# Parts of a weight chunk ahead of the rotations, sample tokens' value products in two halves, and the second row exchange on ScalarE's DMA queue, in the mixer of a two-layer streaming encoder

## The reference

```python
h = layer_norm(DN_ALPHA * h + 0.5 * swiglu(h, gate0, up0, down0), g0, b0)
p = project(h, pos, w_in, ...)      # qa ka va qb kb vb qi ki wi qc kc vc cq ckv kr
#   rope() on qa ka qb kb qi ki kr; va, vb, vc, wi without
h = layer_norm(DN_ALPHA * h + concat(A(h), B(h), C(h), D(h)) @ w_o, g1, b1)
h = layer_norm(DN_ALPHA * h + 0.5 * swiglu(h, gate1, up1, down1), g2, b2)

def rope(x, pos):                   # x1, x2: the halves of a head
    return concatenate([x1 * cos - x2 * sin, x2 * cos + x1 * sin])
```

## Time and profile before

| | |
|---|---|
| median of 3 runs | 1140.57 us (1140.53 to 1141.63) |
| span of the profiled execution | 1139.0 us |
| between span and median | 1.57 us |
| TensorE busy | 1124.5 us, 99% |
| VectorE busy | 692.7 us, 61% |
| ScalarE busy | 542.9 us, 48% |
| granted TensorE clock | 1.000 |
| DMA, mean over the span | 157 GB/s |

### The profile page before, as it was taken

The page is one execution under the profiler, slowest core; times in us unless marked ns, Lnnn a source line. Parts: engine busy times, 40 slices in busy tenths (PEclk is TensorE's granted clock), DMA queues, the critical chain, the costliest instruction groups (busy, mean ns, idle before and its releaser), DMA issues.

```text
span 1139.0 us, 20704 instructions
## 1 busy us (share of the span) xinstructions
PE 1124.5 (99%) x8576; PEld 1092.3 (96%) x8576; DVE 692.7 (61%) x947; ACT 542.9 (48%) x774; POOL 86.4 (8%) x84
## 2 busy tenths in 40 slices
PE   9999999999999999999999999999999999999998
PEld 8999999988899999999999999999888999999997
DVE  5545444779769745445585554467797596454443
ACT  6343343465655634344373434335657564434332
POOL 1000000100151000000100000010003410000001
PEclk9999999999999999999999999999999999999999
DMA  9544445533433545445445544444534325545431
GB/s 349 186 166 167 153 161 167 168 136 107 152 125 122 202 154 179 151 162 167 149 148 189 181 151 172 151 155 131 179 121 145 139 98 199 182 150 169 151 124 42
DMA packets 29555, 179.37 MB, mean 157 GB/s; under 512 B 3824, under 2 KB 3888, under 8 KB 11824
## 3 DMA queue, kind: packets, MB, share of 16 engines
q1 hardware_dynamic: 27744, 172.54, 44.4%
q0 software_dynamic: 1744, 5.88, 1.5%
HBM read 171.79 MB, written 4.25 MB: 155 GB/s over the span
## 4 chain that ended last, share of the span: by engine, by line
PE 76%; DVE 16%; ACT 3%; issue 2%; DMA 1%; SPq 1%; DVEq 0%; ACTq 0%
PE ps L525 24%; PE ps L526 24%; PE ps L527 24%; DVE w_low L1493 2%; ACT w_high L1157 2%; DVE z L1666 2%; DVE w_low L1506 1%; DMA raw<-weights 1%; DVE x_low L1681 1%; DVE z L1656 1%; DVE score L1816 1%; DVE best L1815 1%; DVE zx_low L1646 1%; SPq L417 1%; DVE score L1780 1%
## 5 line engine op out<-in xcount | busy, mean ns | idle before, releaser
L525 PE MATMUL ps<-x_high,w_high 128*128 128x288 f32 x1536 | 457.6, 298 | 2.0 <-DVE w_low L1493 1.3
L527 PE MATMUL ps<-x_high,w_low 128*128 128x288 f32 x1536 | 452.8, 295 | 0.0
L526 PE MATMUL ps<-x_low,w_high 128*128 128x288 f32 x1536 | 452.5, 295 | 0.0
L1493 DVE TENSOR_TENSOR w_low<-raw,w_high 128x2048 fp32r<-128x2048 f32 (+3 forms) x148 | 322.4, 2180 | 212.1 <-ACT w_high L1157 211.6
L1157 ACT ACTIVATE w_high<-raw 128x2048 fp32r<-128x2048 f32 (+2 forms) x166 | 302.9, 1827 | 114.2 <-PE ps L527 107.4
L525 PEld LDWEIGHTS ps<-x_high,w_high 128*128 128x128 f32 x1536 | 288.3, 188 | 8.4 <-DVE w_low L1493 6.2
L527 PEld LDWEIGHTS ps<-x_high,w_low 128*128 128x128 f32 x1536 | 288.4, 188 | 0.0
L526 PEld LDWEIGHTS ps<-x_low,w_high 128*128 128x128 f32 x1536 | 288.1, 188 | 0.2
L527 PE MATMUL ps<-hid_high,w_low 128*128 128x288 f32 x704 | 208.5, 296 | 0.0
L526 PE MATMUL ps<-hid_low,w_high 128*128 128x288 f32 x704 | 208.3, 296 | 0.0
L525 PE MATMUL ps<-hid_high,w_high 128*128 128x288 f32 x704 | 207.7, 295 | 0.0
(11 more groups left out here) (329 smaller groups left out, 1141.4 us busy)
## 6 DMA issues: line engine op xcount, KB each, us to landing
raw<-weights SPq DMA_DIRECT2D x138, 1024.0 KB, 4.9
raw<-weights SPq DMA_DIRECT2D x16, 768.0 KB, 4.3
raw<-weights SPq DMA_DIRECT2D x4, 968.0 KB, 4.7
raw<-weights SPq DMA_DIRECT2D x6, 512.0 KB, 4.0
raw<-weights SPq DMA_DIRECT2D x8, 256.0 KB, 6.2
relu_l<-rope_x SPq DMA_DIRECT2D x24, 72.0 KB, 2.0
out_k<-kT POOLq DMA_DIRECT2D x2, 864.0 KB, 4.7
raw<-weights SPq DMA_DIRECT2D x2, 640.0 KB, 5.4
```

The costliest lines, as they stand in the source:

```text
L525: pe.matmul(out, wh, xh, start=first, stop=False, skip_group_check=True)
L526: pe.matmul(out, wh, xl, start=False, stop=False, skip_group_check=True)
L527: return pe.matmul(out, wl, xh, start=False, stop=last, skip_group_check=True)
L1493: dve.tensor_tensor(wl, r, wh.bitcast(F32), ALU.subtract).then_inc(low_ready, 1)
```

## The change

Four things change in each of the two layers:

- ScalarE makes the high part of chunk base + 4 (`high_until(base + 5)`) right after `hT`, ahead of the wait for `early_scaled` and of the copies to `rope_x`; VectorE makes `fixed_choice` and the low part of that chunk (`low_until(base + 5)`) ahead of both `rope_first`.
- `sample_tokens` is cut in two. The half for chunk base + 2 runs after `token_major(4)` and signals `v_first_ready`; the other half runs where all of it ran.
- The load of chunk base + 5 waits for `v_first_ready` in place of `v_parts_ready`, and stands ahead of the exchange r = 0 in SyncE's order.
- The exchange r = 1 is issued by ScalarE, after its copies to `rope_x`.

```diff
@@ SyncE
-                if local in (TM_AT + NRAW, TM_AT + NRAW + 1):
+                if local == TM_AT + NRAW:
+                    sp.wait_ge(v_first_ready, l + 1)
+                if local == TM_AT + NRAW + 1:
                     sp.wait_ge(v_parts_ready, l + 1)
...
-                        if local == TM_AT + NRAW:
+                        if local == TM_AT + NRAW + 1:
                             turn_rows(l, 0)
-                            turn_rows(l, 1)
@@ helper, called by turn_rows and by ScalarE
+        def swap_blocks(eng, r):
+            for b in range(4):
+                other = b + 1 - 2 * (b % 2)
+                eng.dma_start(turned(r)[32 * b:32 * b + 32], rope_x[32 * other:32 * other + 32, r % 2, :, :])\
+                    .then_inc(rows_turned[r % 2], 16)
@@ TensorE
-                def sample_tokens():
-                    pe.wait_ge(h_ready, KD * event)
-                    for k in range(KD):
+                def sample_tokens(part):
+                    pe.wait_ge(h_ready, KD * event - 4 * (1 - part))
+                    for k in range(4 * part, 4 * part + 4):
...
-                    mm.then_inc(v_parts_ready, 1)
+                    mm.then_inc(v_parts_ready if part else v_first_ready, 1)
...
                 for k in range(3, KD):
                     token_major(k)
-                sample_tokens()
+                    if k == 4:
+                        sample_tokens(0)
+                sample_tokens(1)
@@ ScalarE, mixer
+                high_until(base + 5)
                 act.wait_ge(h_ready, KD * (3 * l + 1))
                 act.wait_ge(early_scaled, early_before(3 * l) + 1)
...
                 to_rope(1, 0)
                 to_rope(1, 1)
-                high_until(base + 5)
+                act.wait_ge(proj_copied, TILES * l + ROPES[1][0] + 2)
+                swap_blocks(act, 1)
@@ VectorE, mixer
                 early_queries(l)
+                fixed_choice()
+                low_until(base + 5)
                 rope_first(l, 0)
-                fixed_choice()
                 rope_first(l, 1)
-                low_until(base + 5)
                 rope_rest(l, 0)
                 rope_rest(l, 1)
```

More of the change, by code:

```diff
@@ L267, in encoder_program @@
         values_copied = sem("values_copied")
+        v_first_ready = sem("v_first_ready")
         v_parts_ready, v_parts_copied, v_added = sem("v_parts_ready"), sem("v_parts_copied"), sem("v_added")
@@ L414, in turn_rows @@
                     sp.wait_ge(roped, ROPED * l + 3)
[L415 to L418, removed]
+                swap_blocks(sp, r)
             for pair in range(4):
```

## The result

The changed kernel takes **1146.25 us** (median of 4, 1145.68 to 1147.0) against 1140.63 for the kernel before beside it: ratio 1.0045, 95% interval 1.0033 to 1.0056, slower by over 0.2%. The forecast was 1142.2, and its range ended at 1143.8. Its profiled execution took 1145.8 us, with a span of 1144.0 and a granted clock of 1.000, as before. The span grew by 5.0 us.

What follows compares the result with a forecast made beforehand. TensorE is busy 99%, so only its waits on the exchange, load and low-part chain could be won. Per layer: tile 4 -0.71, halves +0.15, tile 6 +1.36, sum +0.8; twice that gives 1142.2 us, range 1139.3 to 1143.8.

Steps and rivals of the forecast that it cites:

- The wait before tile 4 goes: TensorE before tile 4: base + 4's low part is ready before it is asked for, winning 0.71 us a layer.
- 0.11 of restart: TensorE at tile 4: second product comes 0.24 after the first, not 0.13; counted as part of the 0.71 us wait.
- The split, +0.15: Sample tokens in two halves: one more change of tile shape and back costs TensorE 0.15 us, bounds 0 and 0.27.
- The load of base + 5 lands at 244.9, since the queue is served in order: SyncE's queue: load issued at 239.9, takes 5.04 us, leaves the path; exchange r = 0 lands after it.
- The exchange r = 0 behind the load, eight exchanges at 0.20 us, whole at 246.5: SyncE's queue: r = 0 shares engines with all eight transfers and is whole at 246.5, making the high part 0.8 us later.
- Break-even at 245.7, each tenth later costs a tenth: Chain to base + 5's high part: r = 0 whole at 245.7 changes nothing; each tenth earlier wins one, later costs one.
- The keys' first copy at 250.8, just in time: Keys' copy before the indexer's logits: done at 250.8, just before TensorE wants it at 251.1.
- rival B: Exchanges cost 0.28 to 0.31 us each, r = 0 whole at 247.1 to 247.4; 1143.4 to 1144.0 us; chance 0.26.
- Costed at nothing: ScalarE's four issues, 0.63 us each, delay the values' copies, still in time for tile 5; base + 6's load goes earlier.
- the share of lone packets counts their latency: Objection to pricing exchanges at the measured share of 0.45 at 108 GB/s, which gives 0.31 us each.
- r = 1 overtakes and the load gives way: DMA engines turn between queues packet by packet, so ScalarE's r = 1 passes r = 0 and all eight transfers count.

Runs made afterwards that it cites:

- two queues, halves: Kernel before with base + 4 parts ahead, sample tokens split, each exchange issued half by SyncE, half by ScalarE, ahead of the load of base + 5: 1139.06 us.
- r = 1 from ScalarE alone: Kernel before with only exchange r = 1 moved to ScalarE, behind its high part of chunk base + 4; old order, sample tokens whole: 1139.38 us.
- two queues, whole: Kernel before with base + 4 parts ahead, each exchange issued half by SyncE, half by ScalarE, ahead of the load; sample tokens unsplit: 1139.66 us.
- r = 0 ahead, halves: Changed kernel with one move: SyncE issues exchange r = 0 ahead of the load of base + 5; sample tokens stay split: 1139.95 us.
- r = 0 ahead, whole: Changed kernel with exchange r = 0 ahead of the load of base + 5 and sample tokens unsplit, so the load waits for all of them: 1139.86 us.
- parts alone: Kernel before with only ScalarE's and VectorE's parts of chunk base + 4 moved ahead of the rotations; queues and products as before: 1142.06 us.
- r = 1 back behind r = 0: Changed kernel with exchange r = 1 back on SyncE, right behind r = 0, both behind the load of base + 5: 1143.92 us.
- transfers of twice the size: Changed kernel with each exchange as two transfers of 64 partitions in place of four of 32, copied straight, so results differ from the reference: 1146.64 us.
- both on ScalarE's queue: Changed kernel with both exchanges issued by ScalarE, r = 0 first, the load of base + 5 alone on SyncE: 1152.24 us.

## Why the prediction was wrong

**The time goes by the high part of base + 5.** For each kernel, the start of the first product with the sines (reading r = 0) and of that high part, both on before's clock, and the time against the kernel before of the same batch:

| kernel | first sines | high part | shift x 2 | time, us |
|---|---|---|---|---|
| before | 244.89 | 250.41 | | |
| two queues, halves | 243.89 | 249.38 | -2.1 | -1.9 |
| r = 1 from ScalarE alone | 244.88 | 249.62 | -1.6 | -1.6 |
| two queues, whole | 243.89 | 249.81 | -1.2 | -1.7 |
| r = 0 ahead, halves | 245.21 | 249.96 | -0.9 | -1.3 |
| r = 0 ahead, whole | 245.24 | 249.98 | -0.9 | -1.1 |
| parts alone | 244.78 | 251.01 | +1.2 | +0.8 |
| r = 1 back behind r = 0 | 247.14 | 251.87 | +2.9 | +2.7 |
| **changed kernel** | 248.45 | 253.18 | +5.5 | +5.6 |
| transfers of twice the size | 248.96 | 253.69 | +6.6 | +5.3 |
| both on ScalarE's queue | 246.49 | 255.18 | +9.5 | +11.0 |

So the frame of the prediction stands: one chain, from the exchange over VectorE's rotations and the keys' copies to this high part, and two layers. Its shift in layer 0, doubled, gives the time within 0.5 us in eight of ten kernels; in the last two rows it is off by 1.3 and 1.5. Layer 1 has the same shifts to 0.3 us (2.5 for 2.8 in the changed kernel), but for both on ScalarE's queue (5.4 for 4.8).

Step by step:

- *The wait before tile 4 goes.* Right that it goes, too much for it. The second product of tile 4 also starts 0.23 us behind the first where nothing is waited for, so the 0.11 of restart that I put to the wait belongs to the tiles' change of shape. With parts ahead and whole samples the way to tile 4 is 6.17 us, before 6.67 (238.36 to 245.03): 0.50 won, not 0.71.
- *The split, +0.15.* Measured 0.32, over my bound of 0.27. I had costed the change of shape at one end of the half only. After it, the successor starts at 239.59, and the next follows after 0.32 in place of 0.22. Together with the first point: TensorE was at tile 4 0.15 us earlier, not 0.55.
- *The load of base + 5 lands at 244.9, since the queue is served in order.* It was issued when forecast (239.8) but took 6.1 us. In the three kernels where exchanges follow it in its queue it took 6.0 to 6.3. The two loads of the earlier trace rows had shown no such thing: the first of them lost nothing. Its data was hardly later than alone (the last packet starts 4.41 us after the issue, 4.31 in the kernel before), and 15 of its 16 reports had come by 245.13; the last one came at 245.91. The high part asks for the load only at 252.97, so by itself this cost nothing. Whether the DMA engine that was last here was also last with the exchange, the records don't say.
- **The exchange r = 0 behind the load, eight exchanges at 0.20 us, whole at 246.5. This is the step that failed.** It was whole at 248.2, on before's clock 248.4, 1.9 us later. All eight were whole at 248.5, 3.7 us after the load would have landed alone (239.77 + 5.04): **0.46 us each**. Two things went into that. In one queue an exchange cost 0.34, near the 0.31 of my upper bound, so 0.20 was the wrong end: filled engines do not move an exchange's bytes at a load's rate. With it, r = 0 is whole at 247.0, as in the run with r = 1 back on SyncE's queue. The other 0.12 each came with ScalarE's queue, and no term of mine had it. In layer 1 it is less, 0.05 each (0.40 against 0.35). Part of it has nothing to do with later loads: 204 of the 256 packets of both exchanges were through before the first packet of the loads issued from 244.85 on started, at 246.12, and up to there a packet took 0.165 us on average, against 0.148 with one queue. The last 52 did share the DMA engines with these loads; how much each part cost is open.
- *Break-even at 245.7, each tenth later costs a tenth.* Right. 248.4 is 2.7 past it; the high part came 2.77 late and tile 6 2.78. The steps between, 3.8 for the rotations and 0.9 for the copies, came out at 4.73 together (248.24 to 252.97).
- *The keys' first copy at 250.8, just in time.* With the exchange 1.9 later it was done 1.9 later, at 252.48 (252.69 on before's clock), and TensorE waited 1.22 for it before the logits. That lies inside the 2.78, as rival B had it.
- *Costed at nothing.* ScalarE's four issues took 3.07 us, one of them 1.15 and not 0.63; the values' copies at 244.23 were still in time. Right.

Right was thus the mechanism of rival B, which had the exchange at 247.1 to 247.4 and 1143.4 to 1144.0 us. That is nearly the run with one queue (247.0, and 1140.57 + 2.65 = 1143.2 us); the changed kernel adds the price of the second queue. The agreement in r = 0 is in part luck: B had all eight exchanges ahead of its end, and there only its own four were. What I held against B, that the share of lone packets counts their latency, does not bear out: the share was the same in a full queue. A row that warned of company was there, outside. The earlier trace rows covers layer 0 alone, and I said of it "no exchange ever over 2.1". The line's row for the kernel before from 806.5 on reads:

```profile
L417 SPq DMA_DIRECT2D relu_l<-rope_x x8: 512/586/592, 836.3 to 862.4; - x8
...
DMA to landing us min/median/max: 1.9/2.1/3.2
```

The 3.2 is the exchange issued at 862.4. Its company is one packet of 16 KB that loads instructions, the only one of another queue from 862 to 866; it holds one DMA engine from 862.8 to 864.4:

```profile
q8 instruction: 1, 0.02, 2.5%
```

Against that, my best evidence for an undisturbed exchange was eight that had the DMA engines to themselves.

Of the two rules that I weighed, that a second issuing engine saves only sequencer time (the Trainium skill, DMA: Bandwidth & Descriptors, Issuing engines are not separate DMA queues) is borne out by one run and not by the other. Without a load in flight that time was worth 1.6 us, since the load stood behind the issues; with one, moving r = 1 won nothing and cost 3.0 us (5.6 less 2.65). The other, turns between queues, fits the landings of r = 0 and r = 1 that alternate. But what I had made of it, that r = 1 overtakes and the load gives way, did not happen: r = 1 was issued from 241.12 on, and its first packet started at 243.95, when the load's were nearly through (the last at 244.18), beside the first of r = 0 at 243.84.

What stays open is why an exchange's bytes go at 237 and not at 419 GB/s. It is neither the size of its packets nor that it reads on-chip memory: the four stores of the result at the end of the kernel before read it too, in packets of the same 2304 bytes, and these take 0.096 us on average where an exchange's take 0.149. Their window, to be read like those of the earlier trace rows (355 GB/s at a share of 0.94):

```profile
1136.00:1137.00 1.00, 0.00 (x0) 0.00 (x0) 0.00 (x0) 0.45 (x2) 0.00 (x0) 1.00 0.94 355
```

Two differences are left, and no run tells them apart: an exchange has both its ends in on-chip memory, and it covers 32 partitions (64 in the run with larger transfers) where loads and stores cover 128. Open, too, is what makes the second queue dear; no run held the two later loads back. Nor is there a run for the split by itself in the kernel before.

## What to carry to other kernels

Price a small transfer by what it meets: ahead of a load these exchanges took 2.0 to 2.4 us, issued while one was in flight mostly 3.2 to 6.1, on the same queue or another. If a short transfer is waited for and a long one is early, the short one goes first, even if that holds the long one up by some us. Then look at the landings of every such transfer in the whole trace, not only of the stretch that is changed, for one that had company.

## Not expected of the hardware

- A load and the small transfers behind it in one queue overlap at their ends: a load alone took 4.8 to 5.1 us, one with exchanges behind it 6.0 to 6.3, and reports of the exchange came before the load's last one (244.78 against 245.91 in the changed kernel). The Trainium skill (DMA: Bandwidth & Descriptors, Two DMAs through the same engine are not ordered) says that descriptors of a queue start in order but are pipelined. The runs fit it but don't prove it: reports do not name their DMA engine, and one engine that is late against the others would look the same.
- With exchanges among the packets the DMA engines were full at 227 GB/s, with loads alone at 419.
- A load that is being served is not interrupted for another queue: in the changed kernel and in the one with both exchanges on ScalarE's queue, an exchange's first packet starts only as the load's last packets do (243.95 and 244.18; 243.68 and 244.06).
- Issuing can grow dearer when two engines issue at once: up to 0.92 us on SyncE and 1.15 us on ScalarE for one transfer, where 0.59 to 0.63 is usual. With two transfers from each engine (the run with twice the size) it did not.
- Going to 128x32 tiles for eight products and back costs TensorE 0.32 us.
